# Eight convolution taps on each side of a panel split, in the retention stage of a two-block transformer kernel

## The chip, the cores and the metric

The kernel runs on one core of a Trainium2 chip. The number that counts is the device time of one execution, in microseconds (us): the median of several runs. A core has a matrix engine (PE, with its weight loads listed apart as PEld), a vector engine (DVE), an activation engine (ACT), a general one (POOL, GpSimd) and a queue that issues transfers (SP). Each has its own program in order, and they meet only in semaphores.

## The reference

The input is one sequence of 512 tokens, 1024 features wide. It goes through two layers of a first block (three kinds of attention and a feed-forward net) and one layer of a second block. The change lies in the second block's mixer, which is, for the 512 tokens and with 256 context tokens feeding the state:

```python
q, k, v, rg, cv, ga, gb = split(u @ w_in)
o = bidir_retention(q, k, v, ...)                 # 4 heads, decayed q.k weights times v
y_ret = (silu(rg) * rms_normed(o)) @ w_ret_out
y = a * sigmoid(g)                                # a, g = split(cv)
y = depthwise_conv(y, 31 taps along the tokens) + conv_b
y_conv = silu(layernorm(y)) @ w_conv_out
h = h + g2 * (sigmoid(ga) * y_ret + sigmoid(gb) * y_conv) @ w_out
```

The convolution is per feature: 8 tiles of 128 features by 512 tokens, each needing 31 multiply-and-add passes (taps) over a 128x512 tile.

## The kernel before

All large products are made in three passes (high by high, low by high, high by low), so each weight panel must be split in a high and a low half before PE may use it. A panel is up to 16 blocks of 128x128. SP streams it into one of two buffers `wraw`; ACT writes the high half `whi` (line 1106); DVE writes the low half `wlo = wraw - whi` (line 1539); for a few panels, among them `("ro", h, 0)`, POOL does both (lines 2088 and 2092). Buffers alternate by the panel's number i: ACT's high half waits for the panel's landing and for PE to have used panel i-2 (`used`); SP's load of panel i waits for the low half of i-2 (`lo`); PE waits for the low half of i in `panel(...)`. So PE uses one panel while the next is split.

The order on each engine is written out by hand. ACT's and DVE's programs call `at(key)`, which splits all panels up to the one after `key`: `at("rg", h, 0)` splits the panel `("rg", h, 1)`, `at("rg", h, 1)` splits `("cv", 2h+1)`.

The retention stage runs over four heads h = 0 to 3. PE's order in a head is: panels q, k, v (two), six rounds of the weights and output products (`ret`: round `kt` uses the decayed weights `Pr` and the values V), with panel `("cv", 2h)` before the rounds; then the two gate panels `("rg", h, 0)` and `("rg", h, 1)`, 48 passes each, with a small sum of squares (line 784) between them; then `("cv", 2h+1)`, `("ro", h, 0)` and `("ro", h, 1)` (product with `w_ret_out`, whose right operand is the gated output, high and low halves `Gh` and `Gl`).

DVE weighs the scores, makes low halves, scales the outputs `O_` (line 1986), multiplies them by silu of the gates (line 1993), makes `Gl` (line 1558) and runs the convolution taps (`conv(n)`, line 1896) in between, where `n` is the number of taps. Counting runs over all tiles: 32 steps for each, the last of which does nothing. POOL adds up the squares of the outputs (line 2109) and does the split for `("ro", h, 0)`.

DVE after the output products of a head, before the change:

```python
conv(16)
for i in range(2):
    at("rg", h, i)
for c in range(4):
    e.wait_ge(ev("rstd", "o", h))
    stt(out=O_[:, c, :], ...)
```

In front of it stand two more `conv(2)`, of the last two rounds, with no wait between them and `conv(16)`.

Of the kernel before, what the change touches and what calls it, by code (L numbers as in the profile page):

```python
# [461 lines left out]
def build(nc, a, out):  # L462
# [4 lines left out]
    with ctx:  # L467
# [11 lines left out]
        def ev(*key):  # L479
            if key not in table:  # L480
                table[key] = Event()
            return table[key]
# [30 lines left out]
        def v(name, i=0, n=1):  # L513
            return vec[:, VOFF[name] + i:VOFF[name] + i + n]
# [1014 lines left out]
        def vector(e):  # L1529
# [3 lines left out]
            def prep(i):  # L1533
                while todo[0] <= min(i, len(stream) - 1):
                    i_, n = todo[0], width(todo[0])
                    todo[0] += 1
                    if i_ not in POOL_LO:
                        e.wait_ge(ev("hi", i_))
                        tt(wlo[i_ % 2][:, 0:n], wraw[i_ % 2][:, 0:n], raw(whi[i_ % 2][:, 0:n]), SUB).then_inc(ev("lo", i_).by(dve_wlo), 1)  # L1539

            def at(*key):
                prep(index[key] + 1)
# [341 lines left out]
            def conv(n):  # L1884
                for _ in range(min(n, 32 * made_tiles[0] - taps[0])):
                    c, k = divmod(taps[0], 32)
                    taps[0] += 1
                    y = YINs.of("y", c)
                    if k == 0:
                        o = CAs.take("cv", c)  # L1890
                        e.wait_ge(o.before, ev("y", "made", c))
                        ts(o.ap, y.ap[:, 0:512], v("convw", CONV_W * c), v("convb", c), MUL, ADD).then_inc(ev("tap", c, 0).by(dve_out), 1)
                    elif k < CONV_W:
                        o = CAs.of("cv", c)
                        e.wait_ge(ev("tap", c, k - 1))
                        stt(out=o.ap, in0=y.ap[:, k:k + 512], scalar=v("convw", CONV_W * c + k), in1=o.ap, op0=MUL, op1=ADD).then_inc(  # L1896
                            ev("tap", c, k).by(dve_out), 1)
                    else:
                        y.free.same(ev("tap", c, CONV_W - 1))
# [22 lines left out]
            for h in range(HEADS):  # L1922
# [54 lines left out]
                for kt in range(6):  # L1977
                    if 0 < kt < 5:
                        weigh(kt + 1)
                    conv(2)  # L1980
                conv(16)
                for i in range(2):
                    at("rg", h, i)
                for c in range(4):
                    e.wait_ge(ev("rstd", "o", h))
# [176 lines left out]
        def sync(e):  # L2162
# [33 lines left out]
            if not e.dry:  # L2196
                e.do.wait_ge(out_stored.sem, 128)

        programs = (tensor, scalar, vector, gpsimd, sync)
        for _ in range(2):  # L2200
            for c in counts:
# [15 lines left out]
        @block.vector  # L2217
        def _(eng):
            vector(Engine(eng))
# [62 lines left out]
```

## Time and profile before

| what | value |
|---|---|
| median of 3 runs | 3170.4 us (3165.24 to 3174.3) |
| the profiled execution, its own time | 3165.67 us |
| its span, first to last instruction | 3163.9 us |
| mean granted clock of PE over the span | 0.989 of full |
| PE busy | 97% of the span |
| DVE, ACT, POOL busy | 48%, 32%, 9% |

The profile records one execution. Busy time is the sum of an engine's instructions; PE's instructions overlap, so its share says little of its pace. A row of the timeline gives the start, the duration, the engine, the line, the operation and, in brackets, how long the engine had stood idle before it and which instruction released it. PE's clock has two levels here, 2.4 GHz (1.00 in the rows) and 1.2 GHz (0.50).

### The profile page before, as it was taken

The numbers are of one execution on the slowest core, as the hardware profiler recorded it, in microseconds if no ns is written. First come the engines' busy times: TensorE is split into PE (matmuls) and PEld (weight loads), VectorE is DVE, ScalarE is ACT, GpSimd is POOL, SyncE is SP. The second block draws the span as 40 slices with busy tenths as digits, with TensorE's granted clock in tenths as the row PEclk, the third lists the DMA queues.
The fourth block names the chain that finished last, engine by engine and source line by source line (L and its number), as shares of the span: only waits on it lengthen the run. The fifth ranks groups of instructions, "written<-read, shape, count | busy, mean of one in ns | idle before, by whom it ended". The sixth has DMA issues, their size and how long they took to land. (4 is left out here: it accounts for less than half of the span.)

```text
span 3163.9 us, 35178 instructions
## 1 busy us (share of the span) xinstructions
PE 3071.1 (97%) x14918; PEld 2463.2 (78%) x14918; DVE 1509.9 (48%) x2260; ACT 1025.0 (32%) x1532; POOL 269.0 (9%) x202
## 2 busy tenths in 40 slices
PE   9999999999999999999999999999999999999998
PEld 6756778877666887878888887778787876778887
DVE  4566333344655334352223325667767774443333
ACT  4543222234533222242121124333333333332222
POOL 0233000021312000000000001010101012000000
PEclk9999999999999999999999999999999999999999
DMA  4114442222124322221111212121212123222222
GB/s 179 42 54 160 156 150 98 93 91 74 49 87 175 144 93 78 96 94 62 72 54 62 78 39 109 40 97 44 97 44 97 44 97 123 94 85 100 94 100 74
DMA packets 45212, 286.15 MB, mean 90 GB/s; under 512 B 5167, under 2 KB 5695, under 8 KB 19584
## 3 DMA queue, kind: packets, MB, share of 16 engines
q1 hardware_dynamic: 42480, 269.77, 23.8%
q0 software_dynamic: 2576, 14.14, 1.2%
q8 instruction: 118, 1.93, 0.2%
q14 instruction: 38, 0.31, 0.0%
HBM read 277.56 MB, written 6.32 MB: 90 GB/s over the span
## 5 line engine op out<-in xcount | busy, mean ns | idle before, releaser
L723 PE MATMUL ps<-A1h,whi 128*128 128x512 f32 x2336 | 931.5, 399 | 49.5 <-DVE wlo L1539 33.4
L724 PE MATMUL ps<-A1l,whi 128*128 128x512 f32 x2336 | 916.5, 392 | 0.0
L725 PE MATMUL ps<-A1h,wlo 128*128 128x512 f32 x2336 | 915.5, 392 | 0.0
L1539 DVE TENSOR_TENSOR wlo<-wraw,whi 128x2048 fp32r<-128x2048 f32 (+2 forms) x220 | 464.4, 2113 | 271.7 <-ACT whi L1106 271.7
L723 PEld LDWEIGHTS ps<-A1h,whi 128*128 128x128 f32 x2336 | 443.5, 190 | 150.4 <-DVE wlo L1539 38.9
L1106 ACT ACTIVATE whi<-wraw 128x2048 fp32r<-128x2048 f32 (+2 forms) x220 | 383.2, 1742 | 471.0 <-PE ps L725 469.2
L725 PEld LDWEIGHTS ps<-A1h,wlo 128*128 128x128 f32 x2336 | 442.4, 189 | 94.2
L724 PEld LDWEIGHTS ps<-A1l,whi 128*128 128x128 f32 x2336 | 443.4, 190 | 88.5 <-issue 1.4
L1716 DVE TENSOR_TENSOR SIL<-SIL,ps 128x512 f32<-128x512 f32 (+1 forms) x110 | 69.8, 634 | 586.3 <-PE ps L725 505.3
L1268 ACT ACTIVATE SIL<-ps 128x512 f32<-128x512 f32 (+1 forms) x110 | 61.0, 554 | 714.0 <-PE ps L725 714.0
L1896 DVE SCALAR_TENSOR_TENSOR CA<-YIN,vec,CA 128x512 f32<-128x512 f32 x240 | 191.2, 797 | 7.3
L723 PE MATMUL ps<-HIDMh,whi 128*128 128x512 f32 x352 | 137.3, 390 | 0.0
L724 PE MATMUL ps<-HIDMl,whi 128*128 128x512 f32 x352 | 137.1, 390 | 0.0
L723 PE MATMUL ps<-HIDh,whi 128*128 128x512 f32 x352 | 137.1, 389 | 0.0
L725 PE MATMUL ps<-HIDh,wlo 128*128 128x512 f32 x352 | 137.0, 389 | 0.0
L724 PE MATMUL ps<-HIDl,whi 128*128 128x512 f32 x352 | 137.0, 389 | 0.0
L725 PE MATMUL ps<-HIDMh,wlo 128*128 128x512 f32 x352 | 136.9, 389 | 0.0
L1169 ACT ACTIVATE PP<-ps,small 128x128 f32<-128x128 f32 (+3 forms) x128 | 67.4, 527 | 116.9 <-DVE small L1614 68.9
L723 PE MATMUL ps<-UC1h,whi 128*128 128x256 f32 x352 | 100.0, 284 | 0.0
L2092 POOL TENSOR_TENSOR wlo<-wraw,whi 128x512 fp32r<-128x512 f32 (+2 forms) x74 | 99.7, 1375 | 1.8
L725 PE MATMUL ps<-UC1h,wlo 128*128 128x256 f32 x352 | 99.6, 283 | 0.0
L724 PE MATMUL ps<-UC1l,whi 128*128 128x256 f32 x352 | 99.6, 283 | 0.0
(363 smaller groups left out, 4244.0 us busy)
## 6 DMA issues: line engine op xcount, KB each, us to landing
wraw<-wstream SPq DMA_DIRECT2D x159, 1024.0 KB, 4.8
MW<-wstream SPq DMA_DIRECT2D x36, 1024.0 KB, 5.0
wraw<-wstream SPq DMA_DIRECT2D x42, 768.0 KB, 4.2
wraw<-wstream SPq DMA_DIRECT2D x34, 640.0 KB, 3.8
wraw<-wstream SPq DMA_DIRECT2D x4, 960.0 KB, 4.7
hk<-gd POOLq DMA_DIRECT2D x1, 2560.0 KB, 15.5
X<-xT SPq DMA_DIRECT2D x4, 512.0 KB, 7.7
sx<-X POOLq DMA_DIRECT2D x1, 2048.0 KB, 6.6
```

Of the source, the lines that this page charges most:

```text
L723: mm(o, l[0], r[0], start=start, stop=False)
L724: mm(o, l[0], r[1], start=False, stop=False)
L725: return mm(o, l[1], r[0], start=False, stop=stop)
L1106: act(whi[i_ % 2][:, 0:n], wraw[i_ % 2][:, 0:n], ACT.Copy, bias=0.0, scale=1.0).then_inc(ev("hi", i_).by(act_whi), 1)
L1169: act(q.ap[:, 0:nk], b.ap[:, 0:nk], ACT.Exp, bias=nm[:, k:k + 1], scale=-1.0, accum_out=le[:, k:k + 1]).then_inc(b.free.by(act_out), 1)
L1268: act(q.ap[:, 0:n], b.ap[:, 0:n], ACT.Silu, bias=0.0, scale=1.0).then_inc(q.full.by(act_out), 1)
L1539: tt(wlo[i_ % 2][:, 0:n], wraw[i_ % 2][:, 0:n], raw(whi[i_ % 2][:, 0:n]), SUB).then_inc(ev("lo", i_).by(dve_wlo), 1)
L1716: tt(q.ap[:, 0:n], q.ap[:, 0:n], b.ap if n == 512 else b.ap[:, 256:512], MUL).then_inc(b.free.by(dve_out), 1)
L1896: stt(out=o.ap, in0=y.ap[:, k:k + 512], scalar=v("convw", CONV_W * c + k), in1=o.ap, op0=MUL, op1=ADD).then_inc(ev("tap", c, k).by(dve_out ...
L2092: last = tt(wlo[i % 2][:, part], wraw[i % 2][:, part], raw(whi[i % 2][:, part]), SUB)
```

## The change

DVE's sixteen taps after the output products are parted: eight stay before the low half of panel `("rg", h, 1)`, eight come between it and the low half of `("cv", 2h+1)`. Nothing else moves, and no engine but DVE has another program. It happens once in each of the four heads.

```diff
                     if 0 < kt < 5:
                         weigh(kt + 1)
                     conv(2)
-                conv(16)
                 for i in range(2):
+                    conv(8)
                     at("rg", h, i)
                 for c in range(4):
                     e.wait_ge(ev("rstd", "o", h))
```

## Rows read from the trace of the kernel before

**Rows 1.** The page's head and its busy times.

```profile
span 3163.9 us, 35178 instructions
PE 3071.1 (97%) x14918; PEld 2463.2 (78%) x14918; DVE 1509.9 (48%) x2260; ACT 1025.0 (32%) x1532; POOL 269.0 (9%) x202
```

**Rows 2.** Waits of PE, 2000 to 2680 us: total, times, longest.

```profile
PE ps L723 <- DVE wlo L1539: 24.8, 6, 5.5
```

**Rows 3.** Timeline of PE, head 1: first gate panel, sum, second, ro.

```profile
2202.36 0.39 PE L723 MATMUL ps<-A1h,whi 128*128 128x512 f32 x1
...
2213.24 1.02 PE L784 MATMUL ps<-tmp_c,mats 128*128 128x512 f32 x2
2219.80 0.79 PE L723 MATMUL ps<-A1h,whi 128*128 128x512 f32 x1 [5.54 <-DVE wlo L1539]
...
2243.07 0.39 PE L723 MATMUL ps<-Gh,whi 128*128 128x512 f32 x1
```

**Rows 4.** The same two places of PE in heads 0, 2 and 3.

```profile
2060.08 0.79 PE L723 MATMUL ps<-A1h,whi 128*128 128x512 f32 x1 [5.53 <-DVE wlo L1539]
...
2084.62 0.39 PE L723 MATMUL ps<-Gh,whi 128*128 128x512 f32 x1
...
2378.26 0.79 PE L723 MATMUL ps<-A1h,whi 128*128 128x512 f32 x1 [5.53 <-DVE wlo L1539]
...
2402.42 0.39 PE L723 MATMUL ps<-Gh,whi 128*128 128x512 f32 x1
...
2536.66 0.73 PE L723 MATMUL ps<-A1h,whi 128*128 128x512 f32 x1 [4.57 <-DVE wlo L1539]
...
2560.16 0.39 PE L723 MATMUL ps<-Gh,whi 128*128 128x512 f32 x1
```

**Rows 5.** Timeline of PE: eight passes of a sum without a wait.

```profile
2663.60 3.60 PE L784 MATMUL ps<-tmp_d,mats 128*128 128x512 f32 x8
```

**Rows 6.** Windows, heads 0, 1: stretch, length, busy times, clock, DMA share, GB/s.

```profile
2053.00:2066.00 13.00, 7.47 (x21) 5.25 (x19) 12.79 (x15) 6.88 (x7) 0.00 (x0) 0.74 0.35 134
2213.00:2224.00 11.00, 5.46 (x16) 3.75 (x15) 10.82 (x12) 6.88 (x7) 0.00 (x0) 0.84 0.28 101
```

**Rows 7.** Timeline of DVE, head 1: all twenty taps, what follows.

```profile
2199.09 18.45 DVE L1896 SCALAR_TENSOR_TENSOR CA<-YIN,vec,CA 128x512 f32<-128x512 f32 x20
2217.46 4.49 DVE L1539 TENSOR_TENSOR wlo<-wraw,whi 128x2048 fp32r<-128x2048 f32 x2
2221.86 2.73 DVE L1986 SCALAR_TENSOR_TENSOR O__114<-O__114,vec,tmp_c 128x512 f32<-128x512 f32 x4
2224.51 1.29 DVE L1993 TENSOR_TENSOR O__114<-O__114,tmp_c 128x512 f32<-128x512 f32 x2
2233.54 1.39 DVE L1558 TENSOR_TENSOR Gl<-O__114,Gh 128x512 fp32r<-128x512 f32 x1 [7.74 <-ACT Gh L1123]
```

**Rows 8.** The same view: the sixth, the twelfth and the last tap.

```profile
2204.72 1.67 DVE L1896 SCALAR_TENSOR_TENSOR CA<-YIN,vec,CA 128x512 f32<-128x512 f32 x1
...
2210.49 0.75 DVE L1896 SCALAR_TENSOR_TENSOR CA<-YIN,vec,CA 128x512 f32<-128x512 f32 x1
...
2216.79 0.75 DVE L1896 SCALAR_TENSOR_TENSOR CA<-YIN,vec,CA 128x512 f32<-128x512 f32 x1
```

**Rows 9.** Waits of DVE, 2000 to 2590 us: total, times, longest.

```profile
DVE Gl L1558 <- ACT Gh L1123: 33.3, 4, 9.0
```

**Rows 10.** Timeline of ACT, head 1.

```profile
2204.66 1.91 ACT L1106 ACTIVATE whi<-wraw 128x2048 fp32r<-128x2048 f32 x1
2213.50 1.91 ACT L1106 ACTIVATE whi<-wraw 128x2048 fp32r<-128x2048 f32 x1 [6.92 <-PE ps L725]
...
2231.71 1.28 ACT L1461 ACTIVATE tmp_c<-ps 128x512 f32<-128x512 f32 x2 [11.24 <-PE ps L725]
```

**Rows 11.** Timeline of POOL, head 1.

```profile
2202.67 4.88 POOL L2109 TENSOR_TENSOR tmp_c<-tmp_c 128x512 f32<-128x512 f32 x3 [18.63 <-ACT tmp_c L1136]
2232.49 1.89 POOL L2088 CAST whi<-wraw 128x2048 fp32r<-128x2048 f32 x1 [24.95 <-PE ps L725]
2234.46 6.71 POOL L2092 TENSOR_TENSOR wlo<-wraw,whi 128x512 fp32r<-128x512 f32 x4
```

**Rows 12.** Issue groups: KB each, median us from issue to landing.

```profile
wraw<-wstream SPq DMA_DIRECT2D x159, 1024.0 KB, 4.8
```

## The prediction

> **What bounds the kernel now.** I began with the page's busy times: PE is busy 97% of the span, DVE under half [rows 1]. A DVE edit can then gain only where PE stands still for DVE, so the next view was the list of PE's waits in the stretch that holds the retention stage. It has one large entry: PE waited 24.8 us in six waits for a low half that DVE makes, the longest 5.5 us [rows 2]. PE's timeline places four of the six. In head 1 the first gate panel starts at 2202.36, the sum of squares at 2213.24, and the second gate panel only at 2219.80, after 5.54 us of idle [rows 3]. Heads 0, 2 and 3 show the same, with 5.53, 5.53 and 4.57 us [rows 4]. That is 21.2 us of the 24.8; the other 3.6 us lie after the fourth head, where the text of the program doesn't change.
>
> Why DVE is late is in its own timeline of head 1 [rows 7]. From 2199.09 it runs twenty taps on end, 18.45 us: the four of the last two rounds and the sixteen of the edited line. Only then, at 2217.46, come the two low halves (4.49 us for both), and PE resumes 2.34 us after the first one started. The high half had been there since 2206.6 [rows 10], so the wait is for the taps and for nothing else.
>
> **What a wait costs beside its idle time.** From the second gate panel's first pass to the first pass with `Gh`, PE has two panels of 48 passes. The first gate panel gives the pace at full clock: 2213.24 - 2202.36 = 10.88 us [rows 3], so two take 21.76 us. Measured are 24.54, 23.27, 24.16 and 23.50 us for heads 0 to 3 [rows 3, 4]: 2.78, 1.51, 2.40 and 1.74 us too long, 8.4 us in all. The granted clock says why: it is 0.74 and 0.84 of full in the stretches around heads 0 and 1 [rows 6], two patterns which heads 2 and 3 repeat. PE stood idle, the clock fell to the lower level, 1.2 GHz, and the first passes after the gap ran at it. There is no other wait between these two points.
>
> The Trainium skill (page "TensorE: Matmul & The Clock Gate", section "Terms") prices this otherwise: the penalty is the throttled time times the share of the clock that is lost. From the clock rows the throttled time is 0.26 x 13 / 0.5 = 6.8 us and 0.16 x 11 / 0.5 = 3.5 us, 20.5 us for the four heads; half of it is an estimate of 10.3 us by that page, and with it the gain below would be 2 us larger. The rows disagree with the page's formula here because part of the low-clock time fell on an idle engine, and the measured 8.4 us is used.
>
> **The first eight taps.** They stay where they are. The first low half follows the twelfth of the twenty taps now instead of the twentieth. Tap 12 starts at 2210.49 and tap 20 at 2216.79 [rows 8]: the low half moves forward by 6.3 us, from 2217.46 to 2211.16. Its high half is there (2206.6). PE would be released at 2211.16 + 2.34 = 2213.50. PE is then still in the sum. How long that takes at full pace comes from the eight passes of another such sum: (3.60 - 1.02) / 6 = 0.43 us a pass [rows 3, 5], so two passes end their turn at 2213.24 + 0.86 = 2214.10. The second gate panel starts there: 5.70 us earlier than now, with 0.6 us to spare. Heads 0 and 2 have the same idle time and so the same margin, head 3 has 1.6 us. The gain is 5.54 + 0.16 each: 5.69 + 5.70 + 5.69 + 4.73 = 21.8 us. With no gap there is no fall of the clock, and the 8.4 us come back too. Bounds: if the whole 0.16 isn't there, 21.2; if the clock penalty stayed in full, 21.8 alone.
>
> **The second eight taps.** They run between the low halves, about 2213.4 to 2219.7 (8 x 0.79). The high half of `("cv", 2h+1)` waits for the end of the first gate panel on PE and takes 2213.50 to 2215.4 [rows 10], no later than now, and is done before these taps. So the second low half runs from 2219.7 to 2222.0, to within 0.1 us where it ends now (2217.46 + 4.49). PE needs it earlier than before: its second gate panel now ends at 2214.10 + 10.88 = 2224.98. The margin is 3.0 us. This is the place where the gain could be given back, and it holds.
>
> **What is late next.** DVE does the same work up to 2222, while PE is 7.2 us ahead of its old times in head 1 (5.70 + 1.51). Behind the low half on DVE stand four scalings of `O_` and two gatings, to 2225.8 [rows 7]; the gating of the third and fourth output waits for silu, which waits for the end of the second gate panel: 2231.71 - 7.2 = 2224.5 [rows 10]. The first `Gl` would then be released at 2233.54 - 7.2 = 2226.3. DVE idled 7.74 us there and will idle 0.5. Over the heads it idled 33.3 us in front of the first `Gl` [rows 9], and PE's advance eats 30.2 of it: 3.1 us stay, none of the four is overdrawn (the largest pair is 9.0 against 8.5). Its cover is thin but real, and behind it lies another: `Gl` is needed only at the ro panel, a whole cv panel of 10.88 us later.
>
> **The moved transfers.** The low half of `("rg", h, 1)` releases the load of `("ro", h, 0)`: issued 6.3 us earlier, at about 2213.5, landed at 2218.3 with 4.8 us from issue to landing [rows 12]. POOL needs it when PE has left the second gate panel, 2225.0, so it is hidden. The low half of cv releases `("ro", h, 1)` as now, at 2222; landed by 2227, needed when PE leaves the cv panel, 2235.9. POOL's split for ro starts when PE frees the buffer, 2232.49 - 7.2, and ends at 2241.17 - 7.2 = 2234.0 [rows 11] against a need at 2243.07 - 7.2 = 2235.9: its 1.9 us of margin shift with it. ACT's program isn't touched, and in the stretch before silu it waits 11.24 us for PE [rows 10]; 4 us of that stay. No wait is added, and SP's queue issues in the same order.
>
> **The sum.** 21.8 + 8.4 = 30.2 us off the profiled execution's own 3165.7 us, whose span is 3163.9: 3135.5. The runs' median is 4.7 us above that execution; taken off the median, the forecast is 3140.2 us, 0.95% faster.
>
> **Rivals.**
>
> (a) *The wait moves to the cv panel in part.* Taps are slow when POOL computes: 1.67 us instead of 0.75 while it adds squares, 2202.67 to 2207.55 [rows 8, 11]. If POOL's work fell on the second eight, they would take 8 x 1.7 = 13.6 us in place of 6.3, the low half would end at 2229.3, and PE would stand 4.3 us plus up to 2.8 us of clock in each head. The gain would fall to about 2 us, and the time to 3168. Against it: POOL has no instruction from 2207.55 until PE leaves the second gate panel. The Trainium skill ("GPSIMD Engine Reference", section "Key points") has GpSimd contend with VectorE instructions that read two SBUF inputs, and a tap reads two; the trace agrees (1.67 against 0.75), but only where both run.
>
> (b) *Only part of the wait goes.* The first gate panel's margin is 0.6 us. If the low half came 1 us later than I place it, PE would stand 0.4 us, three times, and the clock might fall in some heads: 3142 to 3150.
>
> (c) *The gain is given back at the end of the stage.* DVE loses its slack: if the thin 0.5 us in front of `Gl` were overdrawn by 2 us and the taps behind it ran late, PE would meet them at the ro panels and in the gate stage after head 3, where it waits for DVE already (the 3.6 us). Four times 2 us: 3148. Against it, the 10.88 us of the cv panel lie between.
>
> (d) *Slower.* The one mechanism is the low half of cv, behind eight taps that were in front of the other one. It decides from the point where it ends more than 3.0 + 7.5 = 10.5 us later than 2222, so that PE's new wait outweighs the 7.5 us gained per head. At 2 us above that, 4 x 2 = 8 us, it is 3178. Eight taps and a split would have to take 19 us where the rows have 8.5.
>
> (e) *Nothing happens.* PE's wait would have to have another cause than the taps, such as the landing of the panel; but DVE has no wait at all between the twenty taps and the low half [rows 7]. 3170.
>
> **How the numbers follow.** Forecast 0.87; (a) 0.03, (b) 0.05, (c) 0.02, (d) 0.01, (e) 0.02. The range: to the forecast's 3140.2 belong 0.6 us for the passes' overlap, up to 2 us for the clock by either count, and what low-clock stretches later in the kernel cost, whose place may shift against the work: the ones here cost 1.5 to 2.8 us each, so 3 us either way. The larger share is the spread of the runs, 3165.2 to 3174.3, -5 and +4 us. Together 3133 to 3149, which takes in (b). A measurement of this kernel can tell about 0.3%, 9.5 us, from no change. Faster by more: 0.95; within: 0.04; slower: 0.01.
>
> **What would show it.** In the profile of the changed kernel PE's waits for the low half should fall from 24.8 to about 3.6 us, in two waits instead of six, with none in front of the second gate panel; the clock in that stretch should be 1.00; from the sum's start to the first pass with `Gh` it should be 0.86 + 21.76 = 22.6 us in every head; DVE should show twelve taps, a low half, eight taps, a low half; its idle time before the first `Gl` should be some 0.5 us (1.5 in head 3); POOL's split should still end before the ro panel. The prediction is wrong if PE has a new wait at the cv or ro panels, if the sum is followed by a gap, or if low-clock stretches turn up elsewhere in the same number.

## The result, and the profile after

The changed kernel takes 3136.7 us (median of 4 runs, 3135.5 to 3141.0) against 3170.6 us of the kernel before: ratio 0.9897, 95% interval 0.9879 to 0.9914, which is 27 to 38 us. The forecast was 3140.2 us, 30.2 us less than before, in a range of 3133 to 3149.

The page of the kernel after, head and busy times:

```profile
span 3139.2 us, 35178 instructions
PE 3067.2 (98%) x14918; PEld 2460.6 (78%) x14918; DVE 1508.9 (48%) x2260; ACT 1025.3 (33%) x1532; POOL 269.8 (9%) x202
```

PE's waits in the kernel after, 2000 to 2680 us (total, times, longest):

```profile
PE ps L723 <- ACT SGB L1483: 4.4, 1, 4.4
PE ps L784 <- POOL tmp_d L2103: 3.2, 1, 3.2
PE ps L784 <- ACT tmp_d L1136: 2.6, 1, 2.6
PE ps L723 <- DVE wlo L1539: 2.1, 1, 2.1
```

The entry for the low half has gone from 24.8 us in six waits [rows 2] to 2.1 us in one, and that one lies in the gate stage. The other three are not new. The kernel before has the same 4.4 us, at 2694.26, just outside this window, the same 2.6 us, and 2.2 us where it now says 3.2. PE's timeline in head 1 after, at the places of [rows 3]:

```profile
2206.47 1.02 PE L784 MATMUL ps<-tmp_c,mats 128*128 128x512 f32 x2
...
2206.93 0.80 PE L723 MATMUL ps<-A1h,whi 128*128 128x512 f32 x1
...
2229.14 0.39 PE L723 MATMUL ps<-Gh,whi 128*128 128x512 f32 x1
```

No bracket stands behind the sum any more. From the sum's start to the first pass with `Gh` it is 22.67 us, where the kernel before had 29.83. All four heads have 22.66 or 22.67 now, against 31.09, 29.83, 30.71 and 29.09 [rows 3, 4]: 90.67 us in place of 120.72, so 30.05 us are saved there. The two spans differ by 24.7 us only: in this execution the first head's sum starts 1.6 us later (2055.16 against 2053.53), and from the last head's ro panel to the end it is 607.5 us against 603.7. The clock is whole, by windows of 20 us across the same places of heads 0 and 1 (the columns of [rows 6]):

```profile
2050.00:2070.00 20.00, 20.00 (x88) 16.20 (x87) 18.37 (x23) 9.13 (x11) 2.67 (x2) 1.00 0.30 106
2200.00:2220.00 20.00, 20.00 (x88) 16.20 (x87) 18.51 (x21) 8.50 (x10) 2.21 (x2) 1.00 0.29 106
```

DVE in head 1 after, which answers to [rows 7]:

```profile
2192.32 12.14 DVE L1896 SCALAR_TENSOR_TENSOR CA<-YIN,vec,CA 128x512 f32<-128x512 f32 x12
2204.38 2.28 DVE L1539 TENSOR_TENSOR wlo<-wraw,whi 128x2048 fp32r<-128x2048 f32 x1
2206.58 6.26 DVE L1896 SCALAR_TENSOR_TENSOR CA<-YIN,vec,CA 128x512 f32<-128x512 f32 x8
2212.76 2.28 DVE L1539 TENSOR_TENSOR wlo<-wraw,whi 128x2048 fp32r<-128x2048 f32 x1
2214.96 2.73 DVE L1986 SCALAR_TENSOR_TENSOR O__114<-O__114,vec,tmp_c 128x512 f32<-128x512 f32 x4
2217.61 1.29 DVE L1993 TENSOR_TENSOR O__114<-O__114,tmp_c 128x512 f32<-128x512 f32 x2
2220.14 1.06 DVE L1558 TENSOR_TENSOR Gl<-O__114,Gh 128x512 fp32r<-128x512 f32 x1 [1.24 <-ACT Gh L1123]
```

Twelve taps, low half, eight taps, low half. The first low half starts 2.09 us before the sum (2204.38 against 2206.47); before, it started 4.22 us behind it. The idle time in front of the first `Gl` fell from 7.74 to 1.24 us. ACT and POOL in head 1 after, for [rows 10, 11]:

```profile
2218.39 1.21 ACT L1461 ACTIVATE tmp_c<-ps 128x512 f32<-128x512 f32 x2 [4.68 <-DVE O__114 L1993]
```

```profile
2218.55 2.10 POOL L2088 CAST whi<-wraw 128x2048 fp32r<-128x2048 f32 x1 [17.79 <-PE ps L725]
2220.74 6.71 POOL L2092 TENSOR_TENSOR wlo<-wraw,whi 128x512 fp32r<-128x512 f32 x4
```

ACT's silu of the third and fourth gate now waits last for DVE's gating instead of PE, and POOL's split ends at 2227.45, 1.7 us ahead of the ro panel. The first has gone over its edge by some 0.6 us, which the cv panel hides; the second hasn't.

### The profile page after: what moved, and what is told of

Read it like the earlier page. It is cut to its first block and busy times, and to the rows that moved or that the text cites. A ratio compares the mean times of both kernels' runs of the same rounds, so it can differ in the third digit from the quotient of the medians.

```text
span 3139.2 us, 35178 instructions
## 1 busy us (share of the span) xinstructions
PE 3067.2 (98%) x14918; PEld 2460.6 (78%) x14918; DVE 1508.9 (48%) x2260; ACT 1025.3 (33%) x1532; POOL 269.8 (9%) x202
```

## The experiments

Each kernel was run beside the kernel before on the same chip; a ratio is to that. Where microseconds are given for one, they are the ratio's share of the kernel before's 3167 to 3169 us. "The stretch" is the time from the sum's start to the first pass with `Gh`, summed over the heads: 120.72 us before, 90.67 after.

**Twelve and four.**

```diff
                 for i in range(2):
-                    conv(8)
+                    conv(4 if i else 12)
                     at("rg", h, i)
```

> Twelve taps stay before the first low half, four come between. Theory of the record (the wait of PE is tap time, one for one, less 0.6 us of margin): the low half moves forward by 4 x 0.79 = 3.1 us, PE waits 5.5 - 3.1 = 2.4 us in heads 0 to 2 and 1.4 us in head 3, 8.6 us in all, and has no new wait. If the clock falls in a gap of 2.4 us as it does in one of 5.5 us, the penalty stays near 8.4 us and the gain over the kernel before is 12.6 us (ratio 0.996); if it doesn't, the gain is 21 us (0.9934). Rival (the gain is not the wait but the order of the transfers that the low half releases): a gain as large as with eight and eight, ratio 0.990, or none.

Ratio 0.9932 (0.9920 to 0.9945), 21.5 us less than before. PE, heads 0 and 1:

```profile
2056.63 0.50 PE L723 MATMUL ps<-A1h,whi 128*128 128x512 f32 x1 [2.39 <-DVE wlo L1539]
...
2080.14 0.39 PE L723 MATMUL ps<-Gh,whi 128*128 128x512 f32 x1
...
2212.18 0.50 PE L723 MATMUL ps<-A1h,whi 128*128 128x512 f32 x1 [2.39 <-DVE wlo L1539]
...
2234.07 0.39 PE L723 MATMUL ps<-Gh,whi 128*128 128x512 f32 x1
```

The waits are 2.39, 2.39, 2.38 and 1.42 us, as reckoned: four taps moved are 3.1 us of wait less, one for one. The two panels behind take 23.51 us in head 0 and 21.9 in the others: the clock fell at one gap of the four. The stretch is 101.85 us, 18.9 less than before. So the gain follows the wait. The rival's outcomes, a gain as large as with eight and eight or none, both lie outside the interval.

**The changed kernel again.** The same code.

> The changed kernel once more, beside the others on one chip. Theory of the record: ratio 0.9905, 30.2 us; PE's timeline 30.0 us shorter from the first head's sum to the last head's ro panel, as in the first profile. In the first profile 5 us of that were lost outside this stretch (1.6 us before it and 3.7 us behind), while the medians gave 33.9 us. If that loss belongs to the change, this profile shows it again behind the fourth head, in the wait for POOL's sums (3.2 us against 2.2) and in the number of low-clock stretches; if it is the scatter of executions, it comes out otherwise.

Ratio 0.9892 (0.9877 to 0.9907). The stretch is again 22.66 or 22.67 us in each head. From the last head's ro panel to the end of the span it is 604.1 us, where the first profile of the changed kernel had 607.5 and that of the kernel before 603.7. So most of the 3.7 us is scatter. Whether all of it is stays open: the two later profiles of the kernel before (at the end of this section) have 601.5 and 601.7 us there. By the granted clock, 25.0 and 21.5 us of that stretch ran at the low clock in the two profiles of the changed kernel, 16.0 to 16.2 us in the three of the kernel before.

**The gap filled.** The kernel before, with six products of no use in PE's gap (each shows as two passes).

```diff
                         sum_of(OB, ("sq sum", "o", h), 512, ...)
+                        b = PB.take("rg", h, 2)
+                        e.wait_ge(b.before)
+                        for _ in range(6):
+                            mm(b.ap, ones, raw(opU.hi(0)), start=True, stop=True)
```

> The kernel before, with its sixteen taps in one block and its wait, but PE makes six more passes with a matrix of ones and the first tile of u between the sum and the second gate panel, into the bank that this panel overwrites: 6 x 0.86 = 5.2 us of the 5.5 us of gap are filled with work that nothing uses. The second gate panel starts as late as before (the low half decides). Theory of the record: the fall of the clock comes from the idle engine, so it goes and with it 8.4 us: ratio 0.9973. By the reckoning of the Trainium skill's page on the clock gate it would be 10.3 us, ratio 0.9967. Rival (the low clock is no matter of the gap): no change, ratio 1.000, and windows at 0.74 and 0.84 as before.

Ratio 0.9966 (0.9954 to 0.9979), 10.8 us (7 to 15). PE, head 1, and the window over it (line 1074 is the added one):

```profile
2212.01 5.31 PE L1074 MATMUL ps<-A1h,mats 128*128 128x512 f32 x12
2217.71 0.50 PE L723 MATMUL ps<-A1h,whi 128*128 128x512 f32 x1 [0.39 <-DVE wlo L1543]
...
2239.61 0.39 PE L723 MATMUL ps<-Gh,whi 128*128 128x512 f32 x1
```

```profile
2211.00:2222.00 11.00, 10.61 (x35) 6.13 (x34) 10.82 (x12) 6.88 (x7) 0.00 (x0) 1.00 0.29 103
```

The second gate panel starts 6.56 us after the sum, exactly as before (2219.80 - 2213.24), so the wait for the low half is whole; but the clock stays at 1.00 and the two panels take 21.90 us instead of 23.27. The stretch is 113.18 us: 7.5 us less with PE kept busy and nothing else changed. The clock's share of the wait's cost is shown by itself; against the two later profiles of the kernel before it is 8.6 and 8.7 us. The Trainium skill's reckoning (page "TensorE: Matmul & The Clock Gate", section "Terms") gives an estimate of 10.3 us. It is within the interval of the ratio, but above all three traces. The clock's record in the first profile says why: of the 20.5 us at the low clock 3.6 fell while PE still stood idle, and half of the rest is 8.4.

**Eight multiplications more.** The changed kernel, with eight products on DVE that nothing reads.

```diff
                     conv(8)
+                    for _ in range(8 * i):
+                        chain(tt(TC[:, 2, :], YIN[:, 0, 0:512], YIN[:, 0, 0:512], MUL))
                     at("rg", h, i)
```

> The changed kernel with eight more multiplications on DVE behind the second eight taps, into a scratch tile that nothing reads: 8 x about 0.75 = 6.0 us. It doubles what lies between the two low halves. Theory of the record: the second low half has 3.0 us of margin, so PE waits 3.0 us for it in front of the cv panel in each head, 12 us, and the clock falls there at a cost of 0 to 2 us a head: 12 to 20 us slower than the changed kernel, ratio to the kernel before 0.9945 to 0.997. Rival (the margin is much larger, the second block could hold anything): ratio 0.990, as the changed kernel.

Ratio 0.9972 (0.9961 to 0.9982): 3158.0 us against 3134.0 of the changed kernel on the same chip, 24 us slower, more than the 20 at most that was expected. PE, DVE and POOL in head 1:

```profile
2224.05 0.80 PE L723 MATMUL ps<-A1h,whi 128*128 128x512 f32 x1 [4.23 <-DVE wlo L1539]
```

```profile
2214.18 5.77 DVE L1984 TENSOR_TENSOR tmp_c<-YIN 128x512 f32<-128x512 f32 x8
2219.98 4.01 DVE L1539 TENSOR_TENSOR wlo<-wraw,whi 128x2048 fp32r<-128x2048 f32 x1
```

```profile
2219.96 1.89 POOL L2090 CAST whi<-wraw 128x2048 fp32r<-128x2048 f32 x1 [17.78 <-PE ps L725]
```

The margin is there, since 5.8 us were added and PE waits 4.2. But the low half takes 4.01 us instead of 2.28. It was issued just when PE left the second gate panel, and that is the moment POOL's copy for the ro panel starts. Heads 0 and 2 show the same, head 3 doesn't:

```profile
2533.31 2.29 DVE L1539 TENSOR_TENSOR wlo<-wraw,whi 128x2048 fp32r<-128x2048 f32 x1
2534.26 3.10 POOL L2090 CAST whi<-wraw 128x2048 fp32r<-128x2048 f32 x1 [17.95 <-PE ps L725]
2535.66 0.50 PE L723 MATMUL ps<-A1h,whi 128*128 128x512 f32 x1 [1.54 <-DVE wlo L1539]
```

There the low half started 0.95 us before the copy and took its usual 2.29 us, so PE waited 1.54 us and no more; it was the copy that got longer, 3.10 us instead of 1.89.

**POOL held back.** The same, and POOL waits for the second low half.

```diff
                 add_squares(TC[:, 3, :], SQC, ("o", h), 4)
+                e.wait_ge(ev("lo", index["cv", 2 * h + 1]))
                 prep("ro", h, 0)
```

> The kernel with eight more multiplications, and POOL waits for the second low half before it starts its split of the ro panel. In the kernel with eight more, that low half took 4.01 us instead of 2.29, while POOL's copy ran beside it (2219.96 to 2221.85). Theory (POOL, which PE's leaving of the second gate panel lets start, slows the low half that PE then waits for): the low half takes 2.3 us again, PE's wait falls from 4.2 to about 2.5 us in heads 0 to 2, and the kernel is 3 x 1.7 = 5 us faster than the one with eight more, plus what clock comes back: ratio to the kernel before 0.994 to 0.9955 in place of 0.9972. Rival (the low half is slow for another reason, such as the low clock or the transfers of that time): 4.0 us again and the same ratio.

Ratio 0.9959 (0.9946 to 0.9973), 4 us faster than without the added wait, though the two intervals overlap; by the stretches it is 5.4 us (105.57 against 110.93). The ratio is a little worse than expected, the waits are the expected ones:

```profile
2220.90 0.57 PE L723 MATMUL ps<-A1h,whi 128*128 128x512 f32 x1 [2.50 <-DVE wlo L1539]
```

```profile
2212.74 5.77 DVE L1984 TENSOR_TENSOR tmp_c<-YIN 128x512 f32<-128x512 f32 x8
2218.55 2.29 DVE L1539 TENSOR_TENSOR wlo<-wraw,whi 128x2048 fp32r<-128x2048 f32 x1
```

```profile
2220.91 2.35 POOL L2090 CAST whi<-wraw 128x2048 fp32r<-128x2048 f32 x1 [20.15 <-DVE wlo L1539]
```

2.29 us again, and 2.50 us of wait in place of 4.23; head 3 keeps its wait, 1.53 us. That POOL's copy was the cause of the slow low half is shown. Held back, the copy meets the scalings instead, and PE waits 0.5 to 1.5 us at ro panels in every head, where it did so only in head 3 without the added wait.

**Four multiplications more.** As above, with `4 * i`.

> Four more multiplications behind the second eight taps in place of eight: 4 x 0.72 = 2.9 us. Theory of the record (3.0 us of margin in front of the second low half): PE waits 0 to 0.2 us in heads 0 to 2 and not at all in head 3; the time is that of the changed kernel, ratio to the kernel before 0.989 to 0.991. With eight more the wait was 4.2 us, and 2.8 of added work less than 1.4 would be left of it if the margin were smaller: then ratio 0.993.

Ratio 0.9915 (0.9901 to 0.9928). PE doesn't wait at the cv panel in any head, as expected, yet by the ratios the kernel loses 4 to 7 us against the changed one and its equals. Some of these intervals overlap, but PE's timeline bears it out: from sum to sum the first three heads take 152.08, 153.81 and 153.80 us, in the changed kernel 151.31, 151.31 and 151.28, 5.8 us in all; head 3 loses nothing. PE in head 1, at the two ro panels, and DVE:

```profile
2226.12 0.47 PE L723 MATMUL ps<-Gh,whi 128*128 128x512 f32 x1 [0.52 <-issue]
...
2238.74 0.47 PE L723 MATMUL ps<-Gh,whi 128*128 128x512 f32 x1 [1.46 <-DVE YR L2007]
```

```profile
2211.97 2.29 DVE L1539 TENSOR_TENSOR wlo<-wraw,whi 128x2048 fp32r<-128x2048 f32 x1
2214.18 6.51 DVE L1988 SCALAR_TENSOR_TENSOR O__114<-O__114,vec,tmp_c 128x512 f32<-128x512 f32 x4
2220.62 3.47 DVE L1995 TENSOR_TENSOR O__114<-O__114,tmp_c 128x512 f32<-128x512 f32 x2
2225.33 0.69 DVE L1558 TENSOR_TENSOR Gl<-O__114,Gh 128x512 fp32r<-128x512 f32 x1 [1.24 <-ACT Gh L1123]
```

The four scalings take 6.51 us in place of 2.73 and the two gatings 3.47 in place of 1.29, since they now fall beside POOL's split (copy from 2214.86, low half from 2216.84 to 2223.54). So 2.9 us of added work end as 8.9 us of delay: the first `Gl` starts 22.55 us behind the sum (2202.78 here), in the changed kernel 13.67. It ends at 2226.02, and the ro panel, whose first products need it, starts at 2226.12. The profile names no releaser for that wait, so its cause is read from these two times.

**None and sixteen.**

```diff
                 for i in range(2):
-                    conv(8)
+                    conv(16 if i else 0)
                     at("rg", h, i)
```

> No tap stays before the first low half (but for the four of the last two rounds), all sixteen come between the two. Theory of the record: the first low half waits for ACT's high half (ready 3.9 us before the first gate panel has run half), so DVE idles some 4 us there, and the sixteen taps, 12.6 us, follow beside an idle POOL. The second low half ends about 1.7 us later than with eight and eight and keeps 1 to 1.5 us of its margin of 3; the first Gl is late by about 1 us, and the cv panel covers that. No wait of PE, the same time as the changed kernel: ratio to the kernel before 0.990, within 0.001 of the changed kernel's. Rival (DVE has no slack left after the change, so 4 us of its idle time in each head must reach PE): 8 to 16 us slower than the changed kernel, ratio 0.993 to 0.995.

Ratio 0.9902 (0.9888 to 0.9916), as the changed kernel; the stretch is 22.67 us in each head. DVE, head 1 (the sum starts at 2202.15 here):

```profile
2188.01 3.10 DVE L1896 SCALAR_TENSOR_TENSOR CA<-YIN,vec,CA 128x512 f32<-128x512 f32 x4
2195.34 2.56 DVE L1539 TENSOR_TENSOR wlo<-wraw,whi 128x2048 fp32r<-128x2048 f32 x1 [4.23 <-ACT whi L1106]
2197.82 12.55 DVE L1896 SCALAR_TENSOR_TENSOR CA<-YIN,vec,CA 128x512 f32<-128x512 f32 x16
2210.30 2.29 DVE L1539 TENSOR_TENSOR wlo<-wraw,whi 128x2048 fp32r<-128x2048 f32 x1
```

DVE idles 4.23 us for ACT's high half and still the second low half is only 1.86 us later against the sum than with eight and eight (8.15 against 6.29 us): no tap falls beside POOL's squares. The exact parting doesn't matter as long as both low halves stay within their margins. But the 1.86 us already bring the last scaling and both gatings beside POOL's split, and they grow: the first `Gl` comes 19.36 us behind the sum instead of 13.67.

```profile
2221.51 1.72 DVE L1558 TENSOR_TENSOR Gl<-O__114,Gh 128x512 fp32r<-128x512 f32 x1 [1.24 <-ACT Gh L1123]
```

It ends at 2223.23, 1.6 us before the ro panel at 2224.82.

**The second eight left out.** They are not computed, so the output lacks 32 of the 248 taps.

```diff
                 for i in range(2):
-                    conv(8)
+                    if i:
+                        for _ in range(8):
+                            c, k = divmod(taps[0], 32)
+                            ev("tap", c, k).same(ev("tap", c, k - 1))
+                            taps[0] += 1
+                    else:
+                        conv(8)
                     at("rg", h, i)
```

> The second eight taps of each head are not computed at all: 32 of the convolution's 248 taps are missing from the output. Theory of the record: between the low halves they are wholly hidden, so leaving them out is worth nothing: ratio 0.989 to 0.990, as the changed kernel; DVE idles 6.3 us more in front of the second low half or of Gl. Rival (they cost something by holding up the outputs' scaling and so the ro panels): faster than the changed kernel by up to 4 x 2 us, ratio 0.987.

Ratio 0.9894 (0.9880 to 0.9907): worth nothing. The time turns into DVE's waits, in head 1 (the sum starts at 2205.71 here):

```profile
2203.62 2.28 DVE L1539 TENSOR_TENSOR wlo<-wraw,whi 128x2048 fp32r<-128x2048 f32 x1
2207.92 2.29 DVE L1539 TENSOR_TENSOR wlo<-wraw,whi 128x2048 fp32r<-128x2048 f32 x1 [2.01 <-ACT whi L1106]
...
2218.85 1.39 DVE L1558 TENSOR_TENSOR Gl<-O__114,Gh 128x512 fp32r<-128x512 f32 x1 [4.32 <-ACT Gh L1123]
```

**Two heads only.**

```diff
-                    conv(8)
+                    conv((8 if h < 2 else 16) if i == 0 else (8 if h < 2 else 0))
```

> Eight and eight in heads 0 and 1, sixteen in one block in heads 2 and 3. Theory of the record: each head's gain is its own, 8.4 and 7.2 us for heads 0 and 1, no carrying over of DVE's lead or lag to the next head: 15.6 us, ratio 0.9951, with PE's waits of 5.5 and 4.6 us left in heads 2 and 3. Rival (what one head gains the next gives back, or the gain comes from the last heads and the stage behind): less than 8 us or all 30 us.

Ratio 0.9943 (0.9931 to 0.9956), 18 us (14 to 22). The stretches are 22.67, 22.66, 31.12 and 29.11 us, 15.2 less than before, and heads 2 and 3 wait their old 5.54 and 4.57 us. Each head's gain is its own.

**Taps moved into idle time.** A version that builds on the finding: in heads 1 to 3 three taps more are done early in the head, where DVE is idle, and the gate stage behind the heads has nine fewer.

```diff
                     emit(HC, opUC, TC, ("mixc",), ...)
+                conv(5)
                 for i in range(2):
                     rope_out(PB.of("q", h, i), rq, i)
...
                 if f < 6:
-                    conv(12)
+                    conv(9)
```

> The changed kernel, with five taps more in each head in DVE's idle time of 5.3 us in front of the first rope (where tiles allow: 3, 3 and 3 more in heads 1 to 3), and nine instead of twelve in each part of the gate stage behind the heads, so that 18 instead of 27 steps are left for it. Theory of the record (a low half behind a block of taps is PE's wait wherever the taps and the rest exceed a panel's 10.9 us): in the gate stage DVE's work for a panel falls from 13.0 to 10.7 us, PE's wait of 2.1 us for the low half goes; the last tap ends some 9 us earlier and with it the store, the load back and POOL's sums, so the wait of 1 to 3 us for them goes too: 4 to 6 us faster than the changed kernel, ratio to the kernel before 0.987 to 0.988. Rival (the three more taps delay the rope's products and PE waits in the heads): no gain or a loss.

Ratio 0.9873 (0.9858 to 0.9888): 3128.4 us, 40 us under the kernel before and 7 to 10 us under the two kernels above (3138.2 and 3135.5 on the same chip) that equal the changed one. It is faster than both, by more than the 4 to 6 us expected. DVE in the gate stage behind the heads, and PE's sum there, which had waited 3.2 and 1.3 us for POOL in the two profiles of the changed kernel:

```profile
2565.24 7.05 DVE L1896 SCALAR_TENSOR_TENSOR CA<-YIN,vec,CA 128x512 f32<-128x512 f32 x9
2572.21 2.28 DVE L1539 TENSOR_TENSOR wlo<-wraw,whi 128x2048 fp32r<-128x2048 f32 x1
```

```profile
2607.35 1.02 PE L784 MATMUL ps<-tmp_d,mats 128*128 128x512 f32 x2
```

Neither the low half nor POOL's sum holds PE up any more.

**The kernel before, two more profiles.** The same code, unchanged.

> The kernel before, unchanged, for a second profile of it. What it is to tell: the medians of the changed kernel lie 33 to 34 us below those of the kernel before, and the four heads explain 30.1 us in the one profile there is of before. If before's low-clock stretches in the four gaps, or its waits in the gate stage, vary from execution to execution, this profile shows a sum of the four stretches from the sum to the ro panel other than 120.7 us, or a stage behind them other than 603.7 us. Theory: waits of 5.5, 5.5, 5.5 and 4.6 us again to 0.05 us, the clock's share 6 to 10 us; outside the four stretches a scatter of 3 us. Ratio 1.000.

> The same kernel once more, one look: a third profile of the kernel before, for the same question and with the same expectation.

The ratio is 1.0004 (0.9995 to 1.0013) for the first of the two; the second is a single run, 3167.5 us. PE's waits for the low half, 2000 to 2700 us, in either:

```profile
PE ps L723 <- DVE wlo L1539: 23.2, 5, 5.5
```

The four waits are as before to 0.01 us; the stretch is 121.8 and 121.9 us instead of 120.7. With the forecast's 21.8 us taken for the wait itself, the clock's share is 9.4 us where the first profile gave 8.2. The heads then explain 30 to 31 us.

## Why the prediction was right

- **The wait is tap time.** Shown three ways: moving four taps took 3.1 us off it, moving eight took all of it, and each head by itself. Forecast for the idle part 21.8 us.
- **The clock comes back.** Shown by itself with the gap filled: 7.5 us by the trace, 8.4 forecast. The rest of the profile's 30.05 us, 22.5, is the wait, 21.8 forecast. Each term is off by under 1 us, the two errors cancel in part, and that the sum of 30.2 is closer than its terms is luck.
- **The sum's 0.86 us.** Mis-sized. In the changed kernel the second gate panel's first pass starts 0.46 us behind the sum (2206.93 - 2206.47), and the two panels take 22.21 us where 21.76 were reckoned. Why the panels take longer isn't shown. These errors cancel too, again by luck: 22.67 against 22.6 us. So the panel is ready for its low half earlier than the record had it.
- **The margin of the first low half, 0.6 us.** PE shows no gap in any head, but the margin was smaller. The low half ends at 2206.66 and the panel starts at 2206.93, 0.27 us later; in the kernel before PE started 0.05 us after the low half's end, which leaves 0.2 us.
- **The margin of the second low half, 3.0 us.** Confirmed from both sides: 2.9 us more and PE didn't wait there; 5.8 us more and it waited 2.50 us with POOL held back, so the margin is 3.3 us.
- **The second eight are hidden.** Left out, they are worth nothing.
- **Silu and `Gl`.** Mis-sized. The record had the first `Gl` after 0.5 us of idle time (1.5 in head 3), released by PE through silu. Measured: 1.25, 1.24, 1.25 and 1.66 us, and silu was released by DVE's own gating, whose scratch tile it reuses. I had taken silu to wait for PE only. The first `Gl` came 13.7 us behind the sum instead of 13.1. With the second eight left out, PE is the releaser of silu again and `Gl` comes at 13.1 (2218.85 - 2205.71).
- **"Behind it lies another [cover], a whole cv panel."** The cover is there, 9.0 us from the start of the first `Gl` to the ro panel (22.67 - 13.67) and 7.9 from its end, but it is the weak point of the record that it was taken for wide. With none and sixteen, 1.6 us of it were left. With 2.9 us more DVE work the first `Gl` was 8.9 us later and the ro panels waited, 0.5 and 1.5 us. The rival (c), given 2 in 100, is real and lies 1.9 to 2.9 us of DVE work away; its mechanism is that of rival (a), POOL's work beside DVE's, acting on the scalings.
- **Rival (a).** POOL did have nothing to do until PE left the second gate panel. What the rival missed is that a low half issued after PE has left the panel meets POOL's copy, and the wait jumps by 1.7 us. That isn't so for every late one: issued before the copy, as in head 3 with eight more, it took 2.29 us and cost its 1.5 us of lateness alone.
- **The gate stage.** 3.6 us of waits in two were to stay; 2.1 in one did. In the two later profiles of the kernel before it is one as well, so this is scatter and not the change.
- **"Low-clock stretches elsewhere in the same number."** Not in the same number, but there are some. Outside the four stretches the low clock takes 59.1 and 55.6 us of the changed kernel's two profiles and 50.3, 46.8 and 50.3 of the three of the kernel before. In the two equal kernels, none and sixteen and the second eight left out, it is 48.7 and 50.0. Whether the change has a part in it isn't shown.

What stays open: the medians of the changed kernel and of the two versions equal to it lie 31 to 34 us below, the stretches give 30 to 31. The rest is inside each interval, and no run here shows its cause.

## What to carry to other kernels

Work that is hidden in total can still stand in front of the one instruction that the bound engine waits for: look at what the instruction has ahead of it in its own queue, and move only as much as its wait asks for. Count the lower clock after an idle gap as part of the wait's price; here it was 8 us beside 22. And before filling the rest of an engine's idle time, look at which other engine wakes at the same event: here 2.9 us more work, put where it met POOL's, ended as 8.9 us of delay.

## What the runs showed of the hardware

- A DVE low half of 128x2048 took 2.29 us, and 4.01 us when issued 0.02 us behind the start of POOL's copy of 1.89 us. It ended 2.1 us after the copy did, as if it had stood still for the length of the copy. Issued 0.95 us before the copy it took 2.29 us, and the copy took 3.10. The Trainium skill ("SBUF — State Buffer", section "SBUF: two separate sides") describes the port pair that the two engines share as an exclusive lock, with the loser blocked for the other's whole instruction; the trace agrees.
- The low clock doesn't follow every gap. Counted in the four heads: after gaps of 4.57 to 5.54 us it came each time, in three profiles of the kernel before and in two heads with two heads only, and cost 1.5 to 2.9 us against panels at the first gate panel's pace. It came at all three gaps of 4.23 us, at three of the six of 2.38 to 2.51 us, and at none of 1.42 to 1.54 us.
